# Two filler outputs at the head of each attention pass, six over the other fifteen steps

## What is computed

```python
q, k, v = qa[h], ka[h], va[h]                       # 1024 x 128 for each head
z = q @ k.T * 128 ** -0.5
log_keep = where(s < t, log_sigmoid(-z), 0)
suffix = reverse_cumsum(log_keep) - log_keep
w = where(s < t, exp(log_sigmoid(z) + suffix), 0)
out_a = (w @ v) * silu(sb_g)                        # sb_g: a projection of the input
...
merged = sigmoid(m_sb + b) * (out_a @ w_branch_sb) + ...   # m_sb: another projection
```

## Time and profile before

| what | value |
|---|---|
| median of three runs | 3002.91 us |
| the profiled execution, its own time | 3008.91 us |
| its span in the trace | 3007.0 us |
| PE busy | 2810.8 us, 93% of the span |
| DVE busy | 1383.8 us, 46% |
| ACT busy | 960.9 us, 32% |
| the four passes over pairs of heads | from 675.0 to 1089.7 us |
| granted TensorE clock, mean | 0.957 of full |

### The profile page before, as it was taken

The page is one execution under the profiler, slowest core; times in us unless marked ns, Lnnn a source line. Parts: engine busy times, 40 slices in busy tenths (PEclk is TensorE's granted clock), DMA queues, the critical chain, the costliest instruction groups (busy, mean ns, idle before and its releaser), DMA issues.

```text
span 3007.0 us, 35931 instructions
## 1 busy us (share of the span) xinstructions
PE 2810.8 (93%) x14762; PEld 2311.8 (77%) x14762; DVE 1383.8 (46%) x1818; ACT 960.9 (32%) x1567; POOL 140.2 (5%) x231
## 2 busy tenths in 40 slices
PE   5999999998889999987699999998999999999998
PEld 4778888886667778545598677876798998979888
DVE  7565555555556543564324481366324223232232
ACT  6453222336556551112113241233314112021122
POOL 0111111110000001000010000000010000000000
PEclk7999999999999999999899999896799999999999
DMA  2322333240121124321133001000021111111112
GB/s 93 105 89 95 110 110 109 99 162 24 67 84 52 49 74 158 136 91 42 56 111 112 28 1 40 32 29 0 32 88 43 43 57 43 43 57 43 43 49 86
DMA packets 128553, 209.25 MB, mean 70 GB/s; under 512 B 6013, under 2 KB 106538, under 8 KB 124826
## 3 DMA queue, kind: packets, MB, share of 16 engines
q1 hardware_dynamic: 109610, 144.79, 14.3%
q0 software_dynamic: 18800, 62.38, 5.8%
HBM read 161.02 MB, written 46.14 MB: 69 GB/s over the span
## 4 chain that ended last, share of the span: by engine, by line
PE 83%; DVE 7%; ACT 4%; issue 2%; DVEq 1%; DMA 1%; ACTq 1%; SPq 0%; POOL 0%
PE ps L428 22%; PE ps L1854 19%; PE ps L422 19%; PE ps L1951 4%; PE ps L1935 2%; PE ps L2194 2%; PE ps L1910 2%; PE ps L2261 1%; PE ps L2276 1%; PE ps L2007 1%; PE ps L1995 1%; PE ps L2074 1%; PE ps L1921 1%; PE ps L1864 1%; PE ps L2324 1%
## 5 line engine op out<-in xcount | busy, mean ns | idle before, releaser
L407 DVE TENSOR_TENSOR w_lo<-w_raw,w_hi 128x2048 fp32r<-128x2048 f32 x60 | 137.5, 2292 | 410.2 <-ACT w_hi L403 410.2
L403 ACT ACTIVATE w_hi<-w_raw 128x2048 fp32r<-128x2048 f32 x60 | 114.8, 1913 | 591.0 <-DMA w_raw<-in_w_ff 363.6
L428 PE MATMUL ps<-a_hi,w_hi 128*128 128x512 f32 x736 | 294.7, 400 | 4.6 <-issue 3.3
L428 PE MATMUL ps<-a_lo,w_hi 128*128 128x512 f32 x736 | 292.3, 397 | 0.0
L428 PE MATMUL ps<-a_hi,w_lo 128*128 128x512 f32 x736 | 290.2, 394 | 0.0
L422 PE MATMUL ps<-w_lo,f_hi 128*128 128x256 f32 x1024 | 289.8, 283 | 0.0
L422 PE MATMUL ps<-w_hi,f_hi 128*128 128x256 f32 x1024 | 289.8, 283 | 0.0
L422 PE MATMUL ps<-w_hi,f_lo 128*128 128x256 f32 x1024 | 289.8, 283 | 0.0
L1367 DVE TENSOR_TENSOR proj_out<-ps,proj_out 128x512 f32<-128x512 f32 x210 | 141.8, 688 | 240.1 <-PE ps L1854 240.1
L1854 PE MATMUL ps<-t_hi,pw_hi 128*128 128x512 f32 x480 | 196.4, 409 | 4.0 <-DVE t_lo L1341 4.0
L422 PEld LDWEIGHTS ps<-w_hi,f_hi 128*128 128x128 f32 x1024 | 196.6, 192 | 0.2
(11 more groups left out here) (342 smaller groups left out, 5773.0 us busy)
## 6 DMA issues: line engine op xcount, KB each, us to landing
w_raw<-in_w_ff SPq DMA_DIRECT2D x32, 1024.0 KB, 5.4
pw_raw<-in_w_in SPq DMA_DIRECT2D x30, 1024.0 KB, 5.5
projections<-proj_out POOLq DMA_DIRECT2D x88, 256.0 KB, 3.3
w_raw<-in_w_in SPq DMA_DIRECT2D x20, 1024.0 KB, 5.2
projections<-proj_sq POOLq DMA_DIRECT2D x32, 256.0 KB, 2.7
w_raw<-in_w_out SPq DMA_DIRECT2D x8, 1024.0 KB, 5.2
x_in<-in_x SPq DMA_DIRECT2D x8, 512.0 KB, 5.4
q<-projections SPq DMA_DIRECT2D x4, 1024.0 KB, 4.9
```

The costliest lines, as they stand in the source:

```text
L403: act.activation(W_hi[s][:, :, :], W_raw[s][:, :, :], ACT.Copy).then_inc(w_hi, 1)
L407: dve.tensor_tensor(W_lo[s][:, :, :], W_raw[s][:, :, :], W_hi[s][:, :, :].bitcast(f32), ALU.subtract).then_inc(w_lo, 1)
L428: last = pe.matmul(bank[banks[j]][:, :], w[s][:, k, ct * P:(ct + 1) * P], a[:, k, t0 + th * HALF:t0 + (th + 1) * HALF], start=(k == 0 and ...
```

## The change

The first two filler outputs are both issued in step 0, between `scores(2)` and `turn(0)`: 48 matmuls where there were 24. The second of them goes into bank 2, the bank of the attended values; it waits for `kept[0]` of the pass before (signalled at that pass's end), and the first `weigh` of the pass waits until ACT has copied it. ACT copies both outputs in step 1, behind line 978 of that step. The other six outputs end in steps 3, 5, 8, 10, 13 and 15 instead of 4, 6, 8, 11, 13 and 15 (output 1 had ended in step 2).

```diff
-        FILL_ENDS = (0, 2, 4, 6, 8, 11, 13, 15)
-        fill_upto, fill_after = [], {}
-        for J, end in enumerate(FILL_ENDS):
-            first = len(fill_upto)
+        FILL_ENDS = (0, 0, 3, 5, 8, 10, 13, 15)
+        fill_upto, fill_after = [2 * PASSES], {0: (0, 1)}
+        for J in range(2, 8):
+            first, end = len(fill_upto), FILL_ENDS[J]
...
-            fill_after[end] = J
+            fill_after[end] = (J,)
+        FILL_BANK = (3, 2, 3, 3, 3, 3, 3, 3)
...
-                    if S - 1 in fill_after:
-                        keep_filler(fill_after[S - 1])
+                    for J in fill_after.get(S - 1, ()):
+                        keep_filler(J)
...
                     if q >= 1:
                         pe.wait_ge(o_kept, 8 * i + q)
+                    else:
+                        pe.wait_ge(g_raw, 8 * i + 2)
...
-                        if r == 0 and J:
-                            pe.wait_ge(g_raw, 8 * i + J)
+                        if r == 0 and J == 1:
+                            pe.wait_ge(kept[0], n + 1)
+                        elif r == 0 and J:
+                            pe.wait_ge(g_raw, 8 * i + (1 if J == 2 else J))
...
-                        last = pe.matmul(bank[3], w[b][:, k, ct * P:(ct + 1) * P], a[:, k, META + th * HALF:META + (th + 1) * HALF],
+                        last = pe.matmul(bank[FILL_BANK[J]], w[b][:, k, ct * P:(ct + 1) * P], a[:, k, META + th * HALF:META + (th + 1) * HALF],
```

More of the change, by code:

```diff
@@ L970, in keep_filler @@
                         act.wait_ge(pa_stored[J % 2], 32 * i + 16)
-                    act.activation(NB[J][:, :] if J < 4 else stage[J % 2][:, :], bank[3], ACT.Copy).then_inc(g_raw, 1)
+                    act.activation(NB[J][:, :] if J < 4 else stage[J % 2][:, :], bank[FILL_BANK[J]], ACT.Copy).then_inc(g_raw, 1)
                 softplus_terms(0)
```

## The result

The changed kernel took 3026.30 us (median of 9 runs, 3020.56 to 3032.60), the kernel before 3002.91 us (9 runs, 2995.93 to 3017.17). The ratio is 1.0075, 95% interval 1.0056 to 1.0093: slower by 0.75%, more than the 0.5% that the prediction takes as no change. The forecast was 3016.1 us, with no change by that bound as the likeliest case (0.63). The time measured is 0.3 us above the upper end of the range, 3026, and 5 us above that of the rival "clock".

The account below looks back on a forecast made before the run. PE was taken to bound the kernel, with time won or lost only where it waits. Per pass 5.58 - 3.72 + 1.39 + 0.04 = +3.29 us, x 4 = +13.2 us on 3002.91 gave 3016.1 us; range 3004 to 3026.

Parts of the forecast that it names:

- clock: Rival: waits at scores(2) and turn(14) both bring clock falls in two to four passes, +3.4 to +6.8 us, 3021; chance 0.20.
- Start, +5.58 us: Start of a pass: 24 added fillers ahead of turn(0) delay it, scores(3) and turn(1) by 5.58 us.
- Steps 1 to 3: turn(0) to turn(3): 0.93 us less filler work gives nothing back; waits at scores(5), turn(2); shift still +5.58 us.
- Steps 3 to 11: turn(3) to turn(11): 3.72 us of fillers come back, less 1.39 us of net waits around scores(6), (7), (10), (11).
- scores(14), turn(14): turn(11) to turn(14): wait at scores(14) goes, wait at turn(14) grows from 2.49 to 4.35 us; net +0.04 us.
- Sum: All terms together: +3.29 us for a pass, +13.2 us over four passes.
- Small edits at nothing: Second ACT copy in step 1, bank 2 waits, earlier load and store cost nothing; the copy uncovered would cost 2.3 us.
- I take neither more nor fewer of them: one for a pass: TensorE's clock: still one fall to half clock per pass, at turn(14), costing 1.7 us; no added clock cost.
- PE alone: Rival: steps have more slack, waits at scores(6), (10), (11) don't form; about +1.0 us a pass, 3007; chance 0.15.
- Fillers cover the first wait: Rival: leading fillers run in the wait before scores(2), each pass regains 3.45 us, 3002; chance 0.05, including something faster.

Follow-up runs that it names:

- e7: The changed kernel with the second output's 24 fillers issued behind turn(1) in step 1 instead of ahead of turn(0); 3003.90 us, ratio 1.0025.
- e5: The changed kernel plus useless matmuls per pass: 13 before scores(2), ahead of the wait for V, and 15 before turn(14); 3003.81 us, ratio 1.0017.
- e6: The kernel before plus useless matmuls per pass: 13 before scores(2), ahead of the wait for V, and 9 before turn(14); 3005.26 us, ratio 1.0046.
- e11: The kernel before with 14 useless matmuls in step 6 of each pass, where PE doesn't wait; 3020.14 us, ratio 1.0070.
- e10: The kernel before with half of step 0's 24 fillers ahead of scores(2) and the wait for V at the first weigh; 2994.01 us, ratio 0.9986.

## Why the prediction was right and where it fell short

The direction and the mechanism of the order were right, the size of the clock was not.

- **Start, +5.58 us.** turn(0) came 14.7 us behind scores(2) (901.64 to 916.34) against 6.35: 5.6 for the fillers, 2.8 for a fall that the walk didn't have.
- **Steps 1 to 3.** turn(2) 0.90 (about 1.1 said), scores(5) 1.07 (1.1); turn(3), 0.64 before, no longer waits. From turn(0) to turn(3) 12.73 us instead of 12.64. Right; e7 shows the cause.
- **Steps 3 to 11.** scores(6) 0.35 for 0.50, scores(10) 0.61 for 0.74, scores(11) 0.58 for 0.46; scores(7) gone; turn(11) unchanged. From turn(3) to turn(11) 43.98 us instead of 46.61, -2.63 for -2.33 said.
- **scores(14), turn(14).** No wait, and 3.86 for 4.35 us; the walk had missed a wait of 0.22 us at scores(15). From turn(11) to turn(14) both kernels take 17.93 us (+0.04 said).
- **Sum.** 3.29 us a pass said; 2.78 more idle in the third pass, 2.9 to 3.2 between e5 and e6 at full clock. 13.2 us said for the order, some 12 found.
- **Small edits at nothing.** No wait in the trace comes from the second copy, bank 2 or the moved loads; ACT's idle time ahead of step 3's exponential went from 0.69 to 0.15 us.
- **The step that failed: "I take neither more nor fewer of them: one for a pass".** The clock cost 11 to 12 us in all instead of 0. Two parts: the number of falls, as one behind scores(2) came in every pass from the second to the fourth. That was left to a rival at 0.20, against which stood only that three passes of 102.4 us show none there, while the walk made the pass 3.3 us longer. And the price of a fall: 3.42 us of half clock, 1.7 us, was read off the one fall in view, while those of the changed kernel lasted 6.1 and 5.6 us of working time, 3.1 and 2.8 us. That the time measured still lies near the end of the range is luck: the few microseconds added there for the spread of the runs made up for the low price.
- **Rivals.** "Clock" was what happened, and its time, 3021, was 5 us short by the same price. Its reason, that the waits are long enough, is not borne out as a rule: in e7 and e11 the same wait falls in one pass and not in the next. "PE alone": out, the waits are there. "Fillers cover the first wait": rightly put at next to nothing for this change, but its price of 3.45 us was wrong for the kernel before: e10 gained 0.04 us in the third pass, as the wait moved on, and V stood in the way besides.

The Trainium skill ("TensorE: Matmul & The Clock Gate", section "Part 1: The HAM clock gate") says that activity is watched in free-running windows; e7 and e11, where equal waits fell in one pass and not in the next, agree.

## What to carry to other kernels

Before moving work to the head of a step, look at what the other engines have queued behind the instruction it is put in front of: here one transpose held ACT's whole list. A wait seen in a trace may cover an earlier one (V here) and may only move when it is filled, so follow its chain one step further before pricing it. And where a loop has waits of some microseconds, give a fall of TensorE's clock behind each of them a price and a chance whenever the loop's length changes; compare the loop's passes, since the rest of the kernel moves the total.

## What the runs showed that was not expected

- Falls of the clock are of unequal length: 3.4 us of working time at turn(14) before the change, 5.6 and 6.1 us after it, behind waits of 2.5 to 3.9 us. The length of the fall doesn't follow that of the wait: in e11 one of 6 us stands behind a wait of 3.41.
- Although nothing behind the stage was changed, the rest of the kernel took 1900.1 to 1934.2 us in the profiles. PE was busy there for 1784.3 to 1809.2 us with the same 10289 matmuls, and the mean granted clock of the whole executions was 0.951 to 0.965.
